# A hybrid retention and attention step on one core: score steps paired in the attention bodies, and one weight conversion on ScalarE split

## What is computed

```
def diff_attn_block(q, qpos, k, v, kpos, lam):
    s = jnp.einsum('bqhcd,bkhcd->bhcqk', q, k).astype(jnp.float32) * (DIFF_HD ** -0.5)
    visible = (kpos // CHUNK)[None, :] <= (qpos // CHUNK)[:, None]
    s = jnp.where(visible, s, -jnp.inf)
    p = jax.nn.softmax(s, axis=-1)
    a = p[:, :, 0] - lam * p[:, :, 1]
    return jnp.einsum('bhqk,bkhe->bqhe', a.astype(v.dtype), v)
...
q_r, k_r, v_r, g_r, q_d, k_d, v_d, ga, gb = jnp.split(h @ p['w_in'], points, axis=-1)
```

## Time and profile before

| what | before |
|---|---|
| median of 3 runs (lowest to highest) | 2178.83 us (2178.83 to 2179.68) |
| the profiled execution, its span | 2178.79 us, 2177.0 us |
| TensorE matmuls busy | 2160.4 us, 99% of the span |
| TensorE weight loads busy | 2086.2 us, 96% |
| VectorE, ScalarE, GpSimd busy | 56%, 45%, 40% |
| chain that ended last | TensorE 96%, VectorE 2%, ScalarE 1% |

### The profile page before, as it was taken

How to read it: one execution, slowest core, us unless ns; L and a number is a source line. 1 busy time by engine, 2 the same in 40 slices (tenths; PEclk the granted TensorE clock), 3 DMA queues, 4 the chain that set the end, 5 groups by cost and what they waited for, 6 DMA issues and landing times.

```text
span 2177.0 us, 43588 instructions
## 1 busy us (share of the span) xinstructions
PE 2160.4 (99%) x17760; PEld 2086.2 (96%) x17760; DVE 1220.2 (56%) x2109; ACT 984.1 (45%) x1898; POOL 867.0 (40%) x382
## 2 busy tenths in 40 slices
PE   7999999999999999999999999999999999999999
PEld 7889989999999999999998899899999999999999
DVE  7676666656355663266266676665563566523551
ACT  5655554445333542344246555644452335423441
POOL 4244423325343433433463354222353343434433
PEclk9999999999999999999999999999999999999999
DMA  5322232222222222221323232222222222223223
GB/s 170 99 89 95 74 96 90 72 90 82 79 78 98 78 85 82 98 98 60 107 87 98 73 113 94 77 71 71 95 78 89 87 79 97 80 87 98 85 70 112
DMA packets 82550, 193.72 MB, mean 89 GB/s; under 512 B 7760, under 2 KB 37040, under 8 KB 82352
## 3 DMA queue, kind: packets, MB, share of 16 engines
q1 hardware_dynamic: 69632, 182.41, 25.6%
q10 hardware_dynamic: 12720, 8.53, 1.2%
HBM read 177.50 MB, written 13.42 MB: 88 GB/s over the span
## 4 chain that ended last, share of the span: by engine, by line
PE 96%; DVE 2%; ACT 1%; issue 0%; DMA 0%; DVEq 0%; ACTq 0%
PE ps L638 13%; PE ps L640 13%; PE ps L639 13%; PE ps L687 7%; PE ps L688 7%; PE ps L689 7%; PE ps L1064 4%; PE ps L1063 4%; PE ps L1065 4%; PE ps L666 2%; PE ps L825 2%; PE ps L860 2%; PE ps L792 2%; PE ps L784 2%; PE ps L710 2%; PE ps L785 1%
## 5 line engine op out<-in xcount | busy, mean ns | idle before, releaser
L511 POOL TENSOR_TENSOR wlo<-raw,whi 128x1024 fp32r<-128x1024 f32 (+1 forms) x328 | 769.6, 2367 | 1024.8 <-ACT whi L1127 1024.8
L638 PE MATMUL ps<-hl,whi 128*128 128x272 f32 x2432 | 703.0, 289 | 0.0
L640 PE MATMUL ps<-hl,wlo 128*128 128x272 f32 x2432 | 701.0, 288 | 0.0
L639 PE MATMUL ps<-hl,whi 128*128 128x272 f32 x2432 | 699.7, 288 | 0.0
L638 PEld LDWEIGHTS ps<-hl,whi 128*128 128x128 f32 x2432 | 458.7, 189 | 0.0
L640 PEld LDWEIGHTS ps<-hl,wlo 128*128 128x128 f32 x2432 | 457.4, 188 | 0.0
L639 PEld LDWEIGHTS ps<-hl,whi 128*128 128x128 f32 x2432 | 457.1, 188 | 0.0
L1127 ACT ACTIVATE whi<-raw 128x1024 fp32r<-128x1024 f32 (+1 forms) x330 | 313.4, 997 | 203.9 <-PE ps L1065 179.4
L687 PE MATMUL ps<-whi,hl 128*128 128x256 f32 x1216 | 347.7, 286 | 1.4 <-DVE rest L2016 1.4
L688 PE MATMUL ps<-wlo,hl 128*128 128x256 f32 x1216 | 343.0, 282 | 0.0
L689 PE MATMUL ps<-whi,hl 128*128 128x256 f32 x1216 | 342.5, 282 | 0.0
(11 more groups left out here) (243 smaller groups left out, 3352.7 us busy)
## 6 DMA issues: line engine op xcount, KB each, us to landing
raw<-in_w_units_dram SPq DMA_DIRECT2D x260, 512.0 KB, 4.7
raw<-in_w_down_units_dram SPq DMA_DIRECT2D x64, 352.0 KB, 3.4
out_new_k_prompt_dram<-rawk SPq DMA_DIRECT2D x8, 512.0 KB, 3.0
out_new_v_prompt_dram<-vd SPq DMA_DIRECT2D x8, 512.0 KB, 3.0
raw<-in_w_first_dram SPq DMA_DIRECT2D x6, 512.0 KB, 4.7
kc_n<-in_cache_k_dram SPq DMA_DIRECT2D x8, 256.0 KB, 2.8
vc_n<-in_cache_v_dram SPq DMA_DIRECT2D x8, 256.0 KB, 3.7
kc_n<-in_cache_k_dram ACTq DMA_DIRECT2D x8, 256.0 KB, 5.8
```

What stands on the lines that cost most here:

```text
L511: e.tensor_tensor(wlo[:, s, a:b], raw[:, s, a:b], whi[:, s, a:b].bitcast(F32), ALU.subtract).then_inc(*S.up("w_ready", ("lo", j, part)))
L638: e.matmul(out, wh, hi, start=(c == 0), stop=False)
L639: e.matmul(out, wh, lo, start=False, stop=False)
L640: ins = e.matmul(out, wl, hi, start=False, stop=(c == KC - 1))
```

## The change

TensorE's loop becomes a list of steps. Scores 3, 6 and 8 stay about where they were, and 2, 5 and 7 are moved back to stand directly before them; scores 4 and 9 go directly before `weighted(2)` and `weighted(7)`. The shares of the 65 chunks are new. VectorE's `maxes` follow in pairs (`MAXES_BEHIND`), and `sample_sum` stands in turn 4 instead of turn 3. On ScalarE the conversion of the next body's first unit is taken out of `take_filled`, and its halves go behind `turn(3)` and `turn(4)`. No operation is added or removed but one: the two half conversions are now apart.

```diff
--- before.py
+++ after.py
@@ -868,21 +868,36 @@
                                 ins = e.matmul(ps[rows, BANK["o"]:BANK["o"] + HW], aTs[:, c, :], v, start=(c < 2), stop=(c >= NT - 1))
                         ins.then_inc(*S.up("o_ready", (hh, ib)))
 
+                    def step(n, chunks):
+                        fill(chunks)
+                        weighted(n)
+                        if n:
+                            values(n - 1)
+
                     fill(2 * FILL_MID)
                     scores(0)
                     scores(1)
-                    for n in range(10):
-                        if n == 0:
-                            fill(FILL_SHARE[n])
-                        if n + 2 < 10:
-                            scores(n + 2)
-                        if n:
-                            fill(FILL_SHARE[n])
-                        weighted(n)
-                        if n:
-                            values(n - 1)
-                        if n == 5:
-                            cached_keys(1)
+                    step(0, FILL_SHARE[0])
+                    scores(2)
+                    scores(3)
+                    step(1, FILL_SHARE[1])
+                    fill(FILL_SHARE[2])
+                    scores(4)
+                    step(2, 0)
+                    step(3, FILL_SHARE[3])
+                    scores(5)
+                    scores(6)
+                    step(4, FILL_SHARE[4])
+                    step(5, FILL_SHARE[5])
+                    cached_keys(1)
+                    scores(7)
+                    scores(8)
+                    step(6, FILL_SHARE[6])
+                    fill(FILL_SHARE[7])
+                    scores(9)
+                    step(7, 0)
+                    step(8, FILL_SHARE[8])
+                    step(9, FILL_SHARE[9])
                     fill(len(FILL) - filled[0])
                     values(9)
                 for _ in S.bodies("R"):
@@ -1094,7 +1109,8 @@
                 + [("q", t, c) for t in range(NT) for c in range(KC)])
         FILL_FIRST = 18
         FILL_MID = 2
-        FILL_SHARE = (5, 4, 2, 6, 4, 5, 5, 4, 4, 1)
+        FILL_SHARE = (7, 3, 3, 3, 6, 3, 6, 3, 4, 4)
+        MAXES_BEHIND = {1: (2, 3), 2: (4,), 4: (5, 6), 6: (7, 8), 7: (9,)}
         FILL_DONE = {}
         for end in range(1, len(FILL) + 1):
             kind, t, c = FILL[end - 1]
@@ -1262,9 +1278,6 @@
                                 e.wait_ge(*S.own())
                                 e.activation(mer[:, ds(p * 2 + tt // 2, 1), (tt % 2) * HALF:(tt % 2 + 1) * HALF].rearrange("p a b -> p (a b)"),
                                              pv(bank, P, HALF), ACT.Copy).then_inc(*S.up(f"act_free_{bank}", ("ga", tt)))
-                                if tt == 3:
-                                    hi("D", 4, 0)
-                                    hi("D", 4, 1)
                             elif kind == "q":
                                 bank = f"mm{tt % 2}"
                                 e.wait_ge(*S.at("mm_ready", ("N", 3, tt)))
@@ -1346,6 +1359,8 @@
                             e.activation(kcT[:, :], pv("t", P, PAST), ACT.Copy).then_inc(*S.up("act_free_t", ("kc", 1)))
                         take_filled(n)
                         turn(n)
+                        if n in (3, 4):
+                            hi("D", 4, n - 3)
                         if n:
                             out(n - 1)
                         if n + 2 < 10:
@@ -1897,12 +1912,14 @@
                     maxes(1)
                     for n in range(10):
                         combine(n)
+                        if n in (0, 3, 5):
+                            continue
                         if n == NT + 2:
                             e.wait_ge(*S.at("act_free_o", ("o", NT)))
                             sum_of_sample(2 * p, "dve_free_o", "osum")
-                        if n + 2 < 10:
-                            maxes(n + 2)
-                        if ("s", 0) in filled_at(n - 1):
+                        for k in MAXES_BEHIND.get(n, ()):
+                            maxes(k)
+                        if ("s", 0) in filled_at(n - 2):
                             e.wait_ge(*S.at("s_ready", ("q", 1)))
                             sample_sum(rawq[0:DEC, NT, :], "mm1", ("N", 3, 4), "q'")
                 for _ in S.bodies("R"):
```

## The result

| | before | after |
|---|---|---|
| median (lowest to highest) | 2178.95 us (2178.83 to 2179.68, 4 runs) | 2210.49 us (2207.74 to 2213.12, 4 runs) |
| ratio, 95% interval | | 1.0144 [1.0132, 1.0156] |
| the profiled execution, its span | 2178.79, 2177.0 us | 2207.74, 2205.9 us |
| mean granted clock of the profiled execution | 1.000 | 0.997 |
| a body, first score matmul to the next body's | 71.36 us | 75.20 in layer 0, 74.79 in layer 1 |

It is 1.4% slower: the sign was forecast, the size lies above the range (2190 to 2207). The four runs of after spread over 5.4 us, those of before over 0.9.

The account below looks back on a forecast made before the run. The prediction took TensorE's own stream as the bound. Waits of 3.95 us less 1.4 saved made 2.55 us a body, 20.4 in eight, added to 2178.8: 2199.2 us, range 2190 to 2207.

Parts of the forecast that it names:

- The saving: On TensorE, three score stretches less and cheaper steps after scores 4 and 9: 1.4 us a body (1.1 to 1.5).
- The second term: Scores 4 and 9 followed by transpositions instead of wide matmuls: 0.25 us saved a body, between 0 and 0.34.
- The three stretches: Seven score stretches on TensorE become four, each worth 0.39 us: 1.17 us saved a body.
- (b): Query tile 1 waits for bank mm1, freed by VectorE's sample sum, now behind maxima 5 and 6: 2.0 us a body.
- (a): Transpositions 3 wait for VectorE's combination 3, now behind maxima 4: 0.5 us a body.
- (c): Second cached keys wait for turn 5 on ScalarE, delayed by the second half of the weight conversion: 0.65 us a body.
- (e): Combination 8 follows late maxima 9: a wait of 0.2 us a body (0 to 0.4).
- (f): Values 9, with one chunk ahead instead of three, wait for out 8: 0.2 us a body (0 to 0.4).
- (d): Transpositions 6 wait for ScalarE's copy of the second cached keys, behind exponential 7: 0.4 us a body (0.1 to 0.7).
- Rival 5: Each 2 us wait throws TensorE's clock back to half rate, 2.85 us a body on top: 2222 us, chance 0.03.
- Rivals 2, 3 and 4: Only (a) and (b) real, 2187.6 us, chance 0.09; mm1 free in time, 2167.6, 0.04; waits about saving, 2179 to 2183, 0.04.

Follow-up runs that it names:

- experiment 7: Changed kernel with three chunks moved from before transpositions 3 to before query tile 1; 2206.32 us.
- experiment 12: Changed kernel with its named waits mended, first half conversion behind the copy of the cached keys, and maxima 5 ahead of combination 4; 2172.00 us.
- Experiment 5: The kernel of experiment 1 with ScalarE's copy of the second cached keys ahead of exponential 7; 2180.14 us.
- experiment 4: The kernel before with only VectorE's sample sum one turn later, behind maxima 6; 2221.65 us.
- experiment 1: Changed kernel with VectorE's sample sum back behind combination 3, ahead of maxima 5; 2189.23 us.
- experiment 2: Changed kernel with both halves of the last weight conversion back together behind tile 3 of g; 2225.22 us.

## Why the prediction was wrong in size

The order is slower because of the waits, as forecast. Without the clock it would stand at 2206.3 (experiment 7), 7.1 us above the forecast and still inside the range; the clock's part, 4.2 us, which the sum put at nothing, brings the median to 2210.5 and out of it. Step by step:

- **The saving**, 1.4 us forecast, is 1.22 by the changed kernel and 1.24 by experiment 12. The second term, 0.25 for what follows scores 4 and 9, is 0.1. Behind the short scores the first transposition takes 0.14 us instead of 0.11, and the place where they stood before had paid 0.09 us at its second wide matmul, so 0.05 twice. The three stretches are then worth 1.12 to 1.14, where 3 x 0.39 = 1.17 was worked out. By the drain rule of the Trainium skill (TensorEngine Tiling, Key Properties), which gave 1.17, the trace agrees to 0.07.
- **(b)** 2.0 forecast, 2.20 measured with the second matmul behind it: VectorE's chain was read rightly. Taking it away gave back 21.3 us, the clock's part included.
- **(a)** 0.5 and 0.45, **(c)** 0.65 and 0.57, **(e)** and **(f)** 0.2 each and 0.13 and 0.18: as forecast, but (c) only where the clock did not fall.
- **(d)** 0.4 forecast, 1.12 measured, beyond its bound of 0.7: the first failed step. TensorE's side was right (4.2 us from the cached keys), the chain was 5.3 instead of 4.7. It was started at scores 7, but VectorE was not free. GpSimd's timeline (first line) and VectorE's in the last body:

```profile
1404.62 2.36 POOL L511 TENSOR_TENSOR wlo<-raw,whi 128x1024 fp32r<-128x1024 f32 x1 [4.08 <-ACT whi L1143]
...
1406.17 0.17 DVE L1892 RECIPROCAL rinv<-sums 128x2 f32<-128x2 f32 x1 [4.06 <-ACT prob L1305]
1406.37 0.62 DVE L1894 SCALAR_TENSOR_TENSOR rinv<-sums,lam,rinv 128x1 f32<-128x1 f32 x1
1407.03 0.48 DVE L1897 SCALAR_TENSOR_TENSOR prob<-prob,rinv 128x256 f32<-128x256 f32 x1
1407.62 0.61 DVE L1781 TENSOR_TENSOR rt<-ps,rt 32x128 f32<-32x128 f32 x2
...
1408.73 0.17 DVE L1873 MEMSET ps<- 64x128 f32 x1 [0.19 <-PE ps L825]
1408.93 0.96 DVE L1875 TENSOR_REDUCE nmax<-ps 128x2 f32<-128x768 f32 x1
```

  Combination 6 came late behind ScalarE's second half conversion, its small operation took 0.62 us instead of 0.22 and ended with GpSimd's low half (1404.62 + 2.36 = 1406.98), and the other sample sum stands there too. Maxima 7 began at 1408.73 and not, as worked out, 1.5 us behind the keys at 1408.17. (The profile names TensorE for the 0.19 us ahead of it, but scores 7 had ended by 1408.03; VectorE's hand-over to a memset takes 0.19 us elsewhere too, as at 1410.08.) Exponential 7 waited 3.04 us for them, and the copy of the keys stood behind it although it needed none of this. Experiment 5 moved only the copy and got back all 1.1 us.
- **Sum.** 0.72 too little for (d), 0.20 too little for (b) and 0.18 too much saving, less 0.22 that (a), (c), (e) and (f) were put too high: 0.88 us a body, 8 x 0.88 = 7.0. That is the difference of 2199.2 and 2206.3.
- **Rival 5**, given 0.03, is the second failed step, and the one that carried the time out of the range: no part of it stood in the sum. The mechanism is there: behind a wait of 2.1 us the granted clock fell for 3.4 us, in four bodies of the profiled execution. Its price was not the 2.85 us a wait of that rival but 1.5 where nothing covers it (experiment 4) and 0.4 where a later wait does. Only the fastest of the four runs of the changed kernel has a profile; the clocks of the others are 0.998 at 2209.5 us, 0.996 at 2211.5 and 0.994 at 2213.1, against 0.997 at 2207.7. The falls change from run to run, then, and the longest run has the lowest clock, but the mean clock alone does not order the runs. As an estimate, a mean clock of 0.994 is 0.006 x 2210 = 13 us of full clock not granted, which is eight falls of 1.7. That the median's whole 4.2 us over experiment 7 are falls, some of them where nothing covers them, is inferred and not seen. The Trainium skill (TensorE: Matmul & The Clock Gate, Part 1) has the rule that an idle array falls back to half rate; the trace agrees for the waits of 3.3 us, for those of 2.1 us in four bodies of eight, and not for those of 1.5 and less.
- Rivals 2, 3 and 4 are refuted: experiment 1 still has (a), (c) and (d), and with (b) it has a wait of 2.13 us and not a smaller one.

What stays open is why the wait brought the clock down in layer 0 and not in layer 1, where the windows ahead of it read alike; in experiments 2 and 4 it came down in both.

## What to carry to other kernels

Grouping stretches of a narrow mode is worth 0.35 to 0.38 us a stretch here, and it came to 7 us in 2179 only after six other places in the queues of VectorE and ScalarE had been moved. When a chain is walked for a new wait, start it where its engine becomes free, with all that stands in that queue, and look for instructions that wait behind one whose data they do not need: the copy of the keys was such a one, and so was the sample sum. Where TensorE has to wait, two waits of 1.5 and 1.1 us were 4 us cheaper here than waits of 0.4 and 2.1, since the clock stayed up.

## What the runs showed of the hardware

- The granted clock fell to half for about 3.4 us behind a wait of 3.3 us in eight bodies of eight (experiment 4, in three of them for about twice as long), behind a single one of 2.1 us in four of eight, in eight of eight where two of 1.9 to 2.1 us stood in a body (experiment 2), and behind waits of 0.4 to 1.5 us in none (experiments 1, 5, 7).
- An operation of VectorE on 64 numbers took 1.18 us instead of 0.15 while GpSimd's TENSOR_TENSOR on 128x1024 ran, and ended with it. It had two tensors in SBUF as its inputs; the reciprocal ahead of it, with one, kept its 0.16.
